# Moving work between queues in a transformer block: the order of a gate projection, a silu, a transpose, two GpSimd splits and one piece of an output projection

## The reference

```python
h = adaln_pre(x, ...); x = x + 0.5 * (1 + gate0) * swiglu(h, w_ffn1_in, w_ffn1_out)
h = adaln_pre(x, ...)
q, k, v, xc, gate_b, gate_c = split(h @ w_in)          # 6 parts of 512 channels
y_attn = chunked_rel_attention(rms(q), rms(k), v, rel_bias)   # own chunk of 64 and 8 before it
y_conv = gate_b * causal_depthwise_conv(gate_c * xc, w_conv, b_conv)
y = concatenate([rms_norm(y_attn, g_attn_out), rms_norm(y_conv, g_conv_out)])
x = x + (1 + gate1) * (y @ w_out)
h = adaln_pre(x, ...); x = x + 0.5 * (1 + gate2) * swiglu(h, w_ffn2_in, w_ffn2_out)
x = rms_norm(x, g_final)
```

## Time and profile before

| | |
|---|---|
| time, median of 3 runs | 1805.89 us (1805.6 to 1806.16) |
| the profiled execution's own time | 1805.37 us |
| its span, first to last instruction | 1803.6 us |
| mean granted TensorE clock | 0.998 of full speed |
| PE busy | 1775.0 us |
| DVE, ACT, POOL busy | 1177.6, 683.1, 493.3 us |
| mixer of half 0: gate projection, attention loop | from about 783 to 807 us, from 808 to 869 us |
| mixer of half 1: gate projection | from about 1005.5 us |
| first group of the second feed-forward part | to 1198 us |

### The profile page before, as it was taken

The page is one execution under the profiler, slowest core; times in us unless marked ns, Lnnn a source line. Parts: engine busy times, 40 slices in busy tenths (PEclk is TensorE's granted clock), DMA queues, the critical chain, the costliest instruction groups (busy, mean ns, idle before and its releaser), DMA issues.

```text
span 1803.6 us, 21397 instructions
## 1 busy us (share of the span) xinstructions
PE 1775.0 (98%) x8316; PEld 1466.7 (81%) x8316; DVE 1177.6 (65%) x1380; ACT 683.1 (38%) x875; POOL 493.3 (27%) x274
## 2 busy tenths in 40 slices
PE   6999999999999999999999999999999999999997
PEld 6888888888888888877788788888888888888886
DVE  7987776767787585456676576585444444577756
ACT  4442333333334452325344353353233333333443
POOL 1044556644100000205211240324444433310000
PEclk9999999999999999999999999999999999999999
DMA  8146655556856335431244311303422333585633
GB/s 351 39 152 213 227 170 169 188 193 230 338 197 240 100 107 181 139 100 59 88 135 149 119 48 34 131 1 123 138 90 87 99 108 114 192 307 188 232 90 120
DMA packets 87107, 269.89 MB, mean 150 GB/s; under 512 B 8304, under 2 KB 8432, under 8 KB 85488
## 3 DMA queue, kind: packets, MB, share of 16 engines
q1 hardware_dynamic: 82848, 261.20, 42.7%
q10 hardware_dynamic: 4176, 7.60, 1.1%
HBM read 215.81 MB, written 52.95 MB: 149 GB/s over the span
## 4 chain that ended last, share of the span: by engine, by line
PE 93%; issue 3%; DVE 2%; POOL 1%; ACT 1%; DMA 0%; DVEq 0%; SPq 0%; POOLq 0%; ACTq 0%
PE pair L2685 23%; PE pair L2686 23%; PE pair L2687 23%; PE pair L2679 6%; PE pair L2681 6%; PE pair L2680 6%; PE pair L3128 2%; PE pair L3094 2%; PE pair L3109 1%; PE pair L2782 0%; POOL w_lo L996 0%; PE pair L2708 0%; DMA x<-xT 0%; PE pair L2730 0%; DVE acc L1825 0%
## 5 line engine op out<-in xcount | busy, mean ns | idle before, releaser
L2685 PE MATMUL pair<-cb,w_hi 128*128 128x512 f32 x864 | 336.3, 389 | 0.3 <-DVE cb L1848 0.3
L2687 PE MATMUL pair<-cb,w_lo 128*128 128x512 f32 x864 | 336.1, 389 | 0.0
L2686 PE MATMUL pair<-cb,w_hi 128*128 128x512 f32 x864 | 336.1, 389 | 0.0
L2685 PE MATMUL pair<-h_hi,w_hi 128*128 128x512 f32 x824 | 322.5, 391 | 2.5 <-DVE h_lo L1835 2.1
L2686 PE MATMUL pair<-h_lo,w_hi 128*128 128x512 f32 x824 | 321.8, 391 | 0.0
L2687 PE MATMUL pair<-h_hi,w_lo 128*128 128x512 f32 x824 | 321.6, 390 | 0.0
L2685 PEld LDWEIGHTS pair<-cb,w_hi 128*128 128x128 f32 x864 | 162.2, 188 | 34.7 <-DVE cb L1848 0.7
L2687 PEld LDWEIGHTS pair<-cb,w_lo 128*128 128x128 f32 x864 | 162.2, 188 | 33.8
L2686 PEld LDWEIGHTS pair<-cb,w_hi 128*128 128x128 f32 x864 | 162.2, 188 | 33.4
L2685 PEld LDWEIGHTS pair<-h_hi,w_hi 128*128 128x128 f32 x824 | 155.4, 189 | 35.0 <-issue 3.0
L2687 PEld LDWEIGHTS pair<-h_hi,w_lo 128*128 128x128 f32 x824 | 155.4, 189 | 32.6
(11 more groups left out here) (274 smaller groups left out, 3254.4 us busy)
## 6 DMA issues: line engine op xcount, KB each, us to landing
raw<-hs SPq DMA_DIRECT2D x70, 512.0 KB, 3.7
ada_w<-w_ada SPq DMA_DIRECT2D x56, 512.0 KB, 4.3
raw<-w_mix SPq DMA_DIRECT2D x46, 512.0 KB, 3.6
hs<-tt SPq DMA_DIRECT2D x20, 1024.0 KB, 6.4
a<-w_f1o SPq DMA_DIRECT2D x30, 512.0 KB, 6.4
a<-w_f2o SPq DMA_DIRECT2D x30, 512.0 KB, 5.7
ga<-w_f1i SPq DMA_DIRECT2D x22, 512.0 KB, 4.5
ua<-w_f1i SPq DMA_DIRECT2D x22, 512.0 KB, 4.5
```

The lines of the kernel that those rows point to most:

```text
L2685: nc.tensor.matmul(dst, lh, rh, start=first, stop=False, skip_group_check=True)
L2686: nc.tensor.matmul(dst, lh, rl, start=False, stop=False, skip_group_check=True)
L2687: return nc.tensor.matmul(dst, ll, rh, start=False, stop=False, skip_group_check=True)
```

## The change

- Gate projection, both halves: the triple of `ct` = 3, `k` = 0 is issued after the first three triples of `k` = 1, and `h_free`'s first count comes with it.
- `OUT_FILL` loses its last entry, 28. Piece 5 is issued after the loop, ahead of pieces 6 and 7, and DVE's `x_conv(5)` stands between `y_norm2` and `y_low` of the last tile.
- With `mx` = 0, PE's `y_turn` inside the loop stands at s % 8 = 6 and no longer at 5, behind that step's `value_mm`.
- POOL: conv_lo(3) goes ahead of out_lo(2).
- ACT, second feed-forward part: `first_silu1` goes ahead of the four `t2_hi`.

```diff
-        OUT_FILL = (17, 19, 21, 23, 25, 28)
+        OUT_FILL = (17, 19, 21, 23, 25)
...
                     conv_lo(1)
                     conv_lo(2)
+                    conv_lo(3)
                     out_lo(2)
-                    conv_lo(3)
                     out_lo(3)
...
             in_hi(1, 1, 1)
+            first_silu1(1)
             for k in range(KH):
                 t2_hi(1, k)
-            first_silu1(1)
             groups(1)
...
                 y_norm(TT - 1)
                 y_norm2(TT - 1)
+                if mx == 0:
+                    x_conv(5)
                 y_low(TT - 1)
...
+                def gate_mm(ct, k):
+
+                    n = conv_chunk(mx, 8 + ct)
+                    pe.wait_ge(w_ready, n + 1)
+                    return passes(bank[GATE_B[ct]][:], *w_block(mix_slot(n), k), *act_tile(h_hi, h_lo, k),
+                                  k == 0, k == KD - 1)
+
                 pe.wait_ge(qk_done, 8 + 6 * mx)
                 for k in range(KD):
...
                     for ct in range(KA):
-                        n = conv_chunk(mx, 8 + ct)
-                        pe.wait_ge(w_ready, n + 1)
-                        mm = passes(bank[GATE_B[ct]][:], *w_block(mix_slot(n), k), *act_tile(h_hi, h_lo, k),
-                                    k == 0, k == KD - 1)
+                        if ct == KA - 1 and k == 0:
+                            continue
+                        if ct == KA - 1 and k == 1:
+                            gate_mm(ct, 0).then_inc(h_free, 1)
+                        mm = gate_mm(ct, k)
                         if k == KD - 1:
                             mm.then_inc(w_used, 1)
                     if mx == 1 and 1 <= k < 3:
                         qk_turn(5 + k)
-                    if k < KD - 1:
+                    if 0 < k < KD - 1:
                         mm.then_inc(h_free, 1)
...
-                    if s % HEADS == 5 and s > HEADS:
+                    if s % HEADS == (6, 5)[mx] and s > HEADS:
                         y_turn(s // HEADS - 1)
                 value_mm(UNITS - 1)
 
                 if mx == 0:
-                    for i in (6, 7):
+                    for i in (5, 6, 7):
                         pe.wait_ge(xc_done, i - 1)
-                        out_part(OUT_CONV[i], 0, FILL_BANK[i % 2], True, False)
+                        out_part(OUT_CONV[i], 0, FILL_BANK[i % 2], True, i == 5)
                         if i == 6:
                             y_turn(TT - 1)
```

## The result

| | before | after |
|---|---|---|
| median of 7 runs | 1805.89 us (1805.6 to 1807.6) | 1811.67 us (1807.88 to 1812.81) |
| ratio | | 1.0028, 95% interval 1.0019 to 1.0037 |
| the profiled execution's own time | 1805.37 us | 1807.88 us |
| its span | 1803.6 us | 1806.1 us |

The change makes the kernel slower, by 5.8 us between the medians, and the forecast of 1806.8 (1803.4 to 1809.0) was wrong. Two numbers of the table have to be kept apart. The profiled execution after is one of the seven, the fastest, and it is only 2.5 us longer than that of before. The other six took 1810.38 to 1812.81. So the profile shows one part of the cost, and the rest must be looked for in executions that it does not show.

What follows compares the result with a forecast made beforehand. PE, busy 98% of the span, was taken as the bound, so only its waits could be won. Terms -1.4 - 0.6 + 3.6 - 0.7 = +0.9 us, put on the median 1805.89, gave 1806.8 us, range 1803.4 to 1809.0.

Steps and rivals of the forecast that it cites:

- Part 1: Both gate projections: the fourth chunk's low part is used nine matmuls later, so its wait goes, -1.4 us.
- Part 2: POOL's order and the first y_turn: conv_lo(3) no longer delays piece 0, the moved turn costs some, -0.6 us.
- Part 3: Piece 5 behind the loop: ACT's chain through chunk 6 delays the last turn, PE waits 2.9 us, +3.6 us.
- The clock rival: Wait of 2.9 us at the last turn drops PE's clock, fourteen matmuls lose 2.9 us, 1809.7 us; chance 0.10.
- Part 4: Second feed-forward part: the silu fits into ACT's idle hole ahead of t2_hi, PE's wait goes, -0.7 us.
- The small gains are passed on: Rival, all parts: each removed wait is followed by a hidden one, only part 3 stays, about 1809.2 us; chance 0.08.

Runs made afterwards that it cites:

- the run that filled it: Loop's end: seven idle matmuls added to the version with chunk 6's high part late on ACT, 1804.24 us. Wait: twelve added to the changed kernel, 1808.65 us.
- the usual execution: The changed kernel measured again, nothing altered: median 1810.20 us, ratio 1.0023; its profile fell on an execution of 1810.17 us.
- the second set of runs of before: The kernel before, unchanged, run again with each group of follow-up experiments: medians 1805.74, 1805.68 and 1805.67 us.
- the half piece: Changed kernel with chunk 6's high part late on ACT and piece 5 split, six matmuls at step 29, six behind the loop: 1803.12 us, ratio 0.9986.

## Why the prediction was wrong

**Part 1, right.** -1.4 was forecast for the two gates; the profile shows 0.7 at each, the kernel with the gates alone -1.1. No later wait took it back, and SP's later bias loads show no cost.

**Part 2, right in size at its place.** -0.6 forecast and 0.6 found at the first piece, the score pair's wait for DVE included. Costing the later turns of the other tiles at nothing was a little wrong: alone, this part is worth 0.4.

**Part 3, the chain right, its price too low.** Each link came as forecast: high part 3.1 us behind piece 5, turn 8.60 (forecast 8.59), wait 2.87 (2.9). The forecast's times were those of the kernel before, and the first fill piece comes 1.1 us earlier after (839.26 for 840.36). With that added, piece 5 starts at 867.7 (forecast 867.6), the turn at 876.3 (876.2) and piece 7 at 877.0 (876.85), 3.7 us later than before where 3.6 was the term. So where the clock stays full, this part costs what was forecast; the kernel with the piece alone showed 4.1 in its fastest execution (1809.48 beside 1805.37).

**The step that failed** is in the same part: "The 2.8 us of piece 5 are thus taken out of a place where they hid 1.3 us of DVE's latency." That priced the loop's end, left with small matmuls and waits, by its latency alone. In most executions it also costs a fall of the clock, 1.4 us in the trace and 1.3 by the run that filled it. The wait behind it costs a second fall, 1.1 us in the trace and 1.6 by the run that filled it. The clock rival had the right mechanism for the second one and got 0.10; the sign that the prediction itself named for it, matmuls 0.43 us apart behind the last turn, is what the usual execution shows. The argument against it, that the 5.7 us ahead of the wait are dense, did not hold. Its price of 2.9 us in one place was too high for each fall, since in the profile of the change each lasted 3.4 us and the slow start that it was taken from at least 5.7; for the two together it came near: 2.5 to 2.9. So the +3.6 of part 3 was +5.9 in the runs, and these 2.3 us are the largest part of the miss. The silu's 0.7, the gates' 0.3 and the order's 0.2 are the rest of what the runs of the single parts show.

The page's rule that was weighed there (the Trainium skill, TensorE: Matmul & The Clock Gate, HAM oscillation) would have let a wait of this length pass without a fall. The trace of the usual execution disagrees: the clock read 0.51 right behind a wait of 2.85 us, and 0.50 behind a loop's end whose longest single wait was 0.84 us. The measurement decides.

**Part 4, right at its place and worth nothing.** The silu's wait is gone, and the wait for DVE's next low part takes back the 0.7 us. The forecast saw that DVE's sums had room; it did not look at the low part that comes behind them. DVE's work there starts no earlier when the silu does (that low part at 1219.48 before and at 1219.63 with the silu alone). It is long: DVE takes 6.89 us for four instructions of a kind that takes 0.68 with POOL idle, and POOL works beside it. Before the change it was the same, and no run took POOL's work away, so the cause is read from the rows and not tested. The reading agrees with the Trainium skill (GPSIMD Engine Reference, Specifications), which says that the two engines contend when a VectorE instruction has two inputs in SBUF. "The small gains are passed on" was given 0.08 as a rival for all parts; it was true of this part and partly of part 2.

The sum by the runs: -1.1 - 0.4 + 5.9 - 0.0 = +4.4, and the change measured +4.5 beside the second set of runs of before, +5.8 in the first. The two medians of the change differ by 1.5 us, about one fall more, as the mean clocks of the median executions suggest (0.994 and 0.995).

## What to carry to other kernels

When work is taken out of a stretch in which TensorE is already thin, add the clock to the bill: look at what is left of dense matmuls there, and reckon with a fall; here it came in most executions. A profile of one execution can be the one that was spared, so when it is faster than the median of its kernel by 0.1% or more, profile again before explaining. And when a piece of filler has two places to cover, cutting it in two may serve both.

## What had not been expected of the hardware

- The clock fell behind a stretch in which PE was never idle for more than 0.84 us at once. The 3.6 us ahead of that fall, and the same work in the fastest execution of the change, 0.35 us later by its profile:

```profile
862.00:865.60 3.60, 2.15 (x17) 1.65 (x15) 2.27 (x9) 1.28 (x6) 0.54 (x1) 1.00 0.47 146
```

```profile
862.35:865.95 3.60, 2.15 (x17) 1.65 (x15) 2.27 (x9) 1.28 (x6) 0.54 (x1) 1.00 0.52 146
```

PE was busy for 2.15 us in both, and only the first was followed by a fall. So what PE does there makes a fall possible and does not alone decide it; what decides is not shown. With the six matmuls of the half piece in that place PE was busy for 2.45 of 3 us, and no fall came in the profiled execution.

- It does not happen in every execution. The fastest of the change, 1807.88 and 1807.48 us, lie 3.8 and 2.7 us below its medians; the profile of the one has no fall in the loop at all. In the other kernels with falls, too, single executions come out about a fall's price below the rest (1804.31 where the median is 1805.56). The kernel before has the reverse: one of its 26 executions of the second set took 1807.69 us, at a mean clock of 0.996, where the others lie from 1805.37 to 1806.35.
- In the profiles before and after the clock is also at the lower level at the very end, from 1795.7 on, and the change, whose last matmuls come 2 us later, loses 0.7 us on them by it.
- In the traces above, a fall at 866 lasted 3.4 us in three kernels and 6.8 us in one.
